# Two of four sums of weight quarters, made by adding transfers instead of by VectorE

## The reference

```python
h = rms_norm(x, norm_ffn[l])
gate, up = jnp.split(h @ w_gate_up[l], 2, axis=-1)
x = x + (jax.nn.silu(gate) * up) @ w_down[l]
```

## Time and profile before

| | us |
|---|---|
| median of three runs | 1362.07 (1361.05 to 1362.75) |
| the profiled execution, its own time | 1360.11 |
| its span in the trace | 1358.3 |
| PE busy | 1339.5 |
| DVE busy | 849.2 |
| ACT busy | 619.4 |
| POOL busy | 54.1 |

### The profile page before, as it was taken

One profiled execution on the slowest core, in us unless ns is written; L12 is line 12 of the kernel. 1 busy time (PEld: TensorE's weight loads), 2 busy tenths in 40 slices (PEclk: granted clock), 3 DMA queues, 4 the chain that ended last, 5 costly groups with the idle time before them and its releaser, 6 DMA issues. The chain is left out here.

```text
span 1358.3 us, 18018 instructions
## 1 busy us (share of the span) xinstructions
PE 1339.5 (99%) x6941; PEld 1112.0 (82%) x6941; DVE 849.2 (63%) x1313; ACT 619.4 (46%) x1145; POOL 54.1 (4%) x38
## 2 busy tenths in 40 slices
PE   9999999999999999999999999999999999999998
PEld 7888878888888888888788887888798888888886
DVE  5785654457666554344558876767565666666668
ACT  6554333457777533223426466663343332433333
POOL 0025300000000000000010000000000000000000
PEclk9999999999999999999999999999999999999999
DMA  5222213242111154322261200002325412421321
GB/s 168 86 83 81 67 59 114 88 138 80 36 59 61 63 188 151 104 91 66 87 195 61 70 17 16 32 1 78 130 88 168 142 38 87 154 94 63 113 73 62
DMA packets 33622, 120.68 MB, mean 89 GB/s; under 512 B 3716, under 2 KB 5124, under 8 KB 32258
## 3 DMA queue, kind: packets, MB, share of 16 engines
q1 hardware_dynamic: 32962, 118.48, 26.3%
q10 hardware_dynamic: 576, 1.05, 0.4%
HBM read 112.18 MB, written 4.19 MB: 86 GB/s over the span
## 5 line engine op out<-in xcount | busy, mean ns | idle before, releaser
L983 PE MATMUL bank<-a_hi,whi 128*128 128x512 f32 (+1 forms) x880 | 346.9, 394 | 0.4 <-DVE a_lo L2381 0.4
L983 PE MATMUL bank<-a_hi,wlo 128*128 128x512 f32 (+1 forms) x880 | 337.1, 383 | 0.0
L983 PE MATMUL bank<-a_lo,whi 128*128 128x512 f32 (+1 forms) x880 | 336.2, 382 | 0.0
L1431 ACT ACTIVATE whi<-wraw 128x1024 fp32r<-128x1024 f32 x170 | 176.0, 1055 | 195.6 <-PE bank L983 135.1
L1808 DVE TENSOR_TENSOR wlo<-wraw,whi 128x1024 fp32r<-128x1024 f32 x170 | 207.6, 1234 | 60.7 <-ACT whi L1431 54.7
L983 PEld LDWEIGHTS bank<-a_hi,wlo 128*128 128x128 f32 x880 | 165.5, 188 | 32.7
L983 PEld LDWEIGHTS bank<-a_hi,whi 128*128 128x128 f32 x880 | 165.9, 189 | 31.6 <-issue 2.3
L983 PEld LDWEIGHTS bank<-a_lo,whi 128*128 128x128 f32 x880 | 165.9, 189 | 31.1 <-issue 1.7
L983 PE MATMUL bank<-arena 128*128 128x128 f32 (+5 forms) x1332 | 184.9, 284 | 3.0 <-DVE arena L2032 1.5
L983 PEld LDWEIGHTS bank<-arena 128*128 128x128 f32 (+1 forms) x1332 | 163.9, 190 | 13.0 <-issue 5.3
L983 PE MATMUL bank<-whi,a_hi 128*128 128x512 f32 x288 | 115.6, 401 | 1.5 <-DVE wlo L1808 0.7
(11 more groups left out here) (272 smaller groups left out, 1866.5 us busy)
## 6 DMA issues: line engine op xcount, KB each, us to landing
wraw<-in_wblk SPq DMA_DIRECT2D x170, 512.0 KB, 3.8
arena<-in_quarters SPq DMA_DIRECT2D x8, 1024.0 KB, 7.1
arena<-in_quarters SPq DMA_DIRECT2D x4, 768.0 KB, 6.1
arena<-in_x SPq DMA_DIRECT2D x4, 512.0 KB, 6.1
arena<-in_x SPq DMA_DIRECT2D x1, 2048.0 KB, 7.7
spill<-arena SPq DMA_DIRECT2D x4, 512.0 KB, 7.8
arena<-spill SPq DMA_DIRECT2D x1, 2048.0 KB, 9.3
out<-arena SPq DMA_DIRECT2D x8, 256.0 KB, 2.0
```

The costliest lines, as they stand in the source:

```text
L983: return nc.tensor.matmul(o, lhsT, rhs, start=start, stop=stop, **kw)
L1431: A(whi[n % 2][:, cols], wraw[i][:, 0:cols.stop - cols.start], ACT.Copy).then_inc(s_hi, 1)
```

## The change

The signs of the scheme are turned so that all sums of weights become plus: t1 = b11 + b12, t3 = b12 + b22, t2 = t1 + b22, t4 = t2 + b21. SP copies b11 into the slot of t1 and b12 into the slot of t3 (COPIED); then POOL issues, for each, a transfer that adds another quarter from memory onto the slot, b12 onto t1 and b22 onto t3 (ADDED), once the copy has landed. b11, b21 and b22 are copied for themselves as well. t2 and t4 stay with DVE. The minus signs move into `hsplit` (one add and one subtraction swapped) and into `take` (which subtracts products 6 and, once, 7, and no longer product 4).  There are five copies and two adding transfers in a group instead of four copies. The copies of t1 and t3 stand together where b11's stood, b11's where b12's stood.

```diff
-QUARTERS = ("b11", "b12", "b21", "b22")
-SUMS = ("t1", "t2", "t3", "t4")
+QUARTERS = ("b11", "b21", "b22", "t1", "t3")
+COPIED = {"b11": 0, "b21": 2, "b22": 3, "t1": 0, "t3": 1}
+ADDED = {"t1": 1, "t3": 3}
+SUMS = ("t2", "t4")
...
-            sums = {6: [("tsum", group, 2)], 7: [("tsum", group, 3)]}.get(p, [])
+            sums = [("tsum", group, 1)] if p == 7 else []
...
-LAST_OF = {"b12": 7, "b22": 3, "b21": 4}
+LAST_OF = {"t1": 5, "t3": 7, "b22": 3, "b21": 4}
...
-    for c, name in zip(range(e - 4, e) if e - a == 8 else (e - 3, e - 3, e - 2, e - 1), ("b11", "b12", "b22", "b21")):
+    for c, name in zip((e - 4, e - 4, e - 3, e - 2, e - 1) if e - a == 8 else (e - 3, e - 3, e - 2, e - 2, e - 1),
+                       ("t1", "t3", "b11", "b22", "b21")):
...
-                    if name in QUARTERS:
+                    if name in ADDED:
+                        act.wait_ge(s_added[name], 16 * group + 16)
+                    elif name in QUARTERS:
                         act.wait_ge(s_raw[name], 16 * group + 16)
...
-                link(v.tensor_tensor(hsum[:, 0, :], a21, a22, ALU.add))
+                link(v.tensor_tensor(hsum[:, 0, :], a21, a22, ALU.subtract))
                 link(v.tensor_tensor(hsum[:, 1, :], hsum[:, 0, :], a11, ALU.subtract))
-                v.tensor_tensor(hsum[:, 3, :], a12, hsum[:, 1, :], ALU.subtract).then_inc(s_hsum, 1)
+                v.tensor_tensor(hsum[:, 3, :], a12, hsum[:, 1, :], ALU.add).then_inc(s_hsum, 1)
...
-                out_, left, right = (("t1", "b12", "b11"), ("t2", "b22", "t1"), ("t3", "b22", "b12"), ("t4", "t2", "b21"))[i]
+                out_, left, right = (("t2", "t1", "b22"), ("t4", "t2", "b21"))[i]
...
+            def add_quarters(n):
+
+                for group, name in QUARTERS_AT.get(n, ()):
+                    if name in ADDED:
+                        pool.wait_ge(s_raw[name], 16 * group + 16)
+                        cols = slice(0, width(PRODUCT_AT[group, 1]))
+                        pool.dma_start(raw[name][:, cols], dram["quarters"][4 * group + ADDED[name]][:, cols],
+                                       accum_op=ALU.add).then_inc(s_added[name], 16)
+
             for s in STEPS:
+                if s[0] == "gemm" and s[2] == 0:
+                    add_quarters(s[1])
```

More of the change, by code:

```diff
@@ L74 @@
 PAIR = {1: 0, 6: 0, 7: 0, 4: 0, 2: 1, 5: 1, 3: 1}
+SUBTRACTED = {(6, (0, 1)), (7, (1, 1))}
 TAKES = {1: ((0, 0),), 2: ((0, 0),), 6: ((0, 1),), 5: ((1, 1),), 7: ((1, 0), (1, 1)), 3: ((0, 1),), 4: ((1, 0),)}
-QUARTERS = ("b11", "b12", "b21", "b22")
-SUMS = ("t1", "t2", "t3", "t4")
+QUARTERS = ("b11", "b21", "b22", "t1", "t3")
+COPIED = {"b11": 0, "b21": 2, "b22": 3, "t1": 0, "t3": 1}
+ADDED = {"t1": 1, "t3": 3}
+SUMS = ("t2", "t4")
 def weave(*streams, weights=None):
@@ L293, in plan @@
             f = ff(c, a, whole)
-            sums = [("tsum", group, 0)] if c == e - 2 else []
-            steps += f[:2] + untaken + H(*unsplit) + f[2:4] + sums + f[4:]
+            steps += f[:2] + untaken + H(*unsplit) + f[2:]
             untaken, unsplit = [], [c]
-        steps[-2:-2] = [("tsum", group, 1)]
+        steps[-2:-2] = [("tsum", group, 0)]
         made = products(group, (e - a) // 2)
@@ L756, in emit @@
         hsq = mem(4, [512])
-        raw = {name: mem(kb, [BLK]) for name, kb in (("b11", 0), ("b12", 8), ("b21", 16), ("b22", 24), ("t1", 32))}
-        raw.update(t2=raw["b11"], t3=raw["b12"], t4=raw["b21"])
+        raw = {name: mem(kb, [BLK]) for name, kb in (("b11", 0), ("t3", 8), ("b21", 16), ("b22", 24), ("t1", 32))}
+        raw.update(t2=raw["b11"], t4=raw["b21"])
         half_chunk = T // 2
@@ L844, in emit @@
         s_tsum = sem("s_weights_summed")
+        s_added = {name: sem("s_quarter_added_" + name) for name in ADDED}
         s_h, s_hsum, s_hround = sem("s_hidden_made"), sem("s_hidden_summed"), sem("s_hidden_rounded")
@@ L918, in _ @@
                     cols = slice(0, width(PRODUCT_AT[group, 1]))
-                    src = dram["quarters"][len(QUARTERS) * group + QUARTERS.index(name)]
+                    src = dram["quarters"][4 * group + COPIED[name]]
                     sp.dma_start(raw[name][:, cols], src[:, cols]).then_inc(s_raw[name], 16)
@@ L1964, in tsum @@
                 r = {name: ap[:, cols] for name, ap in raw.items()}
-                out_, left, right = (("t1", "b12", "b11"), ("t2", "b22", "t1"), ("t3", "b22", "b12"), ("t4", "t2", "b21"))[i]
+                out_, left, right = (("t2", "t1", "b22"), ("t4", "t2", "b21"))[i]
                 for name in (left, right):
-                    if name in QUARTERS:
+                    if name in ADDED:
+                        dve.wait_ge(s_added[name], 16 * group + 16)
+                    elif name in QUARTERS:
                         dve.wait_ge(s_raw[name], 16 * group + 16)
@@ L1970, in tsum @@
                         dve.wait_ge(s_tsum, len(SUMS) * group + SUMS.index(name) + 1)
[L1971 to L1977, removed]
+                dve.wait_ge(s_lo, 2 * PRODUCT_AT[group, 1 if out_ == "t2" else 2] + 2)
+                v.tensor_tensor(r[out_], r[left], r[right], ALU.add).then_inc(s_tsum, 1)
             def take(n):
@@ L1987, in take @@
                         x = x2[:, 2 * rows_half + t, 512 * cols_half:512 * cols_half + 512]
-                        last = v.tensor_tensor(x, x, bank[BANK[g]][:, :], ALU.subtract if b["product"] == 4 else ALU.add)
+                        last = v.tensor_tensor(x, x, bank[BANK[g]][:, :],
+                                               ALU.subtract if (b["product"], (rows_half, cols_half)) in SUBTRACTED else ALU.add)
                     last.then_inc(s_end["V"], 1)
```

## The result

The change makes the kernel slower by a third of a percent: 1366.66 us median (1363.81 to 1367.25, ten runs) against 1360.95 (1359.7 to 1362.75, ten runs) beside it, ratio 1.0035, 95% interval 1.0025 to 1.0045. The forecast of no change was wrong; the price lies near that of the first rival. (The prediction's base of 1362.07 was a median of three runs, 1.1 us above the one of ten.)

What follows compares the result with a forecast made beforehand. PE was taken as the bound, busy 99% of the span. Terms for sums, signs, waits for adds and late weight pieces were all 0, so 1360.1 us profiled, 1362.1 for the median, forecast as 1362.0; range 1359.6 to 1366.5.

Steps and rivals of the forecast that it cites:

- the first rival: First group: adds cost three copies or more, weight pieces come late, PE waits 4.8 us, 1366.9 us; chance 0.11.
- What bounds the kernel: Feed-forward: PE, busy 99% of the span, never late until deep in the last group; only 2.0 us of waits there.
- DVE's relief is worth 0: Six removed weight sums, 12.7 us of DVE's time, lie beside PE's work: worth 0, at best 0.1 us.
- Signs 0: Additions for subtractions in `hsplit`, the sums and `take`: same instruction, same shape, 0.
- POOL's queue outside the span 0: Around the span 1.8 us lie now; nothing added, against a rival of another 1 to 3 us, chance 0.03.
- The wait for the adds is covered by 41 us: First group: t1 has at least 41 us to be made; two transfers take at most 28 us; price 0.
- An add costs two copies of engine time, 6.1 us: DMA engines: an add must read the slot besides what a copy does, so twice a copy's 3.06 us.
- The slack of the weight pieces: Block PE begins at 1050.77: second piece may be 5.1 us late, first 7.5; next block's 4.9 and 5.5.
- At 3.6 us of overhang it holds: 1030 to 1060 us: 15.3 us of added engine work exceeds 11.7 us free by 3.6, within the pieces' slack.
- 0 (weight pieces late): Term of the sum for SP's weight pieces delayed by the added bytes in all groups: 0 us.
- Two of the prediction's own signs of being wrong: PE wait for `wlo` between 1040 and 1075 us, DMA share near 1.0 there; third was DVE idle before line 1980.
- The rival "weight pieces late": First group: overhang 9.8 us less slack of about 5, PE waits 4.8 us, giving 1366.9 us; chance 0.11.

Runs made afterwards that it cites:

- e3: The change with its adding transfers left out, so both sums missing, five copies a group and two DVE sums remaining: 1360.42 us, ratio 1.0002.
- e1: The change, but the first group's two adds wait until DVE has made the rests of chunk 6's and chunk 7's weights: 1360.32 us, ratio 0.9999.
- e2: The change with both adding transfers of each group replaced by plain copies from the same queue at the same place: 1359.86 us, ratio 1.000.
- e7: The change, but in the first group the add onto t3 waits until the rests of chunk 7's weights are made: 1360.56 us, ratio 0.9996.
- e8: The change with b11's copy moved behind chunk 5's weight pieces in the first two groups: 1365.23 us, ratio 1.0029.
- e6: The kernel before, without adds; SP holds chunk 4's second weight piece until PE has ended chunk 3's block: 1367.08 us, ratio 1.0048.
- e4: The change, but the add onto t3 waits until the add onto t1 has landed: 1366.45 us, ratio 1.004.
- e5: The change with only the first group's adds; those of the second and third group left out: 1364.52 us, ratio 1.0029.

## Why the prediction was wrong

- *What bounds the kernel, and that DVE's relief is worth 0*: right (e3: 1.0002; 316.24 us without a gap before, in e1 and in e3). The six sums that went had lain beside PE's work.
- *Signs 0*: right (e1). *POOL's queue outside the span 0*: nearly. Around the span lie 1.8 to 1.9 us in e1, as before, but 2.2 in the change and 2.1 to 2.2 in e2, e7 and e8; what makes these 0.3 to 0.4 us is open.
- *The wait for the adds is covered by 41 us*: right. The adds landed after at most 15.8 us, and neither DVE's six instructions of line 1980 nor ACT ever waited for one.
- *An add costs two copies of engine time, 6.1 us*: about right, 5.1 to 6.2. The page "Collectives: The Full Stack" of the Trainium skill, section "The bandwidth ceiling: the fold count and why AG ≠ RS ≠ AR", finds about half a copy's rate for the adding step of a collective, as it reads two sources; these runs agree (1.7 to 2.1 copies).
- *The slack of the weight pieces, 5.1 us for chunk 4's second and 7.5 for its first*: right. e7 was 3.6 us late with the second and lost nothing; the change was 9.5 us late with it and PE waited 3.9 us, and 7.7 us late with the first, where PE waited 0.3.
- *"At 3.6 us of overhang it holds"*, and with it the term "0 (weight pieces late)": this step failed. It took the extra work of the engines over 30 us, took off the free share of all 30 us, and compared the rest with the slack of one piece. Of the 11.7 us free, 7.4 lay behind 1044 us, when the piece had all but landed, and only 0.9 in the 6 us in which it was on its way. What counts here is the work outstanding when the piece is issued: by the rough sum some 16 us in the change instead of 6 before (two pieces of 1.5 and a quarter of 3). Landing went from 6.1 us to 15.6, that is 9.5 later; less the slack of 5.1, 4.4, and PE waited 3.9 + 0.3. The first rival supposed in the same way that some of the lateness falls on the adds, "which nobody misses"; the small, urgent piece landed with the second add, not ahead of it. Two of the prediction's own signs of being wrong came: a PE wait for `wlo` at 1053 us, and a DMA share of 1.00. That transfers of SP and POOL share the same engines the Trainium skill says (page "DMA: Bandwidth & Descriptors", section "Issuing engines are not separate DMA queues"), and the trace agrees (with POOL's adds beside it SP's piece took 15.6 us instead of 6.1); the prediction had that rule, but not its price at one moment.
- *The rival "weight pieces late"* had mechanism, place and nearly the price: 1366.9 against 1366.66, by a sum that was right by chance. It put an add at three copies, where two do, started from a base 1.1 us too high, and had neither the clock (1.5 us in the profiled execution) nor what comes with a wait beyond its length.

Why SP's piece ends last and not by its own size is not settled. Beside plain transfers of POOL it landed late too (e2, 10.6 us), so it is nothing of the adding alone; what the adding does is to make the backlog longer. No run looks into the order within the engines.

## What to carry to other kernels

Cost an added transfer at the moment when the next urgent one is issued: sum the engine time of all that is outstanding then, and compare the end of it with the last moment at which that one may land; here that was good to some 2 us. A mean share over tens of microseconds hides a burst. A transfer that nobody waits for soon should wait for a quiet stretch by a semaphore that exists already; here two such waits removed the loss. And relief for an engine for which PE never waits was worth nothing here, so it may not cost anything either.

## What was not expected of the hardware

- An adding transfer of 1 MB took 5.1 to 6.2 us of all 16 engines and 8.7 to 15.8 us to land; a plain one from the same queue took 2.9 us of them and 5.1 to 10.5 us to land (e2).
- The full engines moved 254 GB/s with adds among them and 434 GB/s without.
- A single wait of PE costs more than its length in some executions. After the new wait of 3.9 us the granted clock was at half for about 3.3 us, after the 5.6 us of e6 for about 6.9, and after the 3.7 us of e4 it fell too; after e4's 1.6 us and e5's 1.7 us it did not. In the change and in e6 the fall cost PE 1.5 us. Of the ten executions of the change seven had a mean clock of 0.997; of the kernel before it was seven of 29 in one set and seven of 25 in the other. The old wait of 1.9 us in the last group was followed by such a fall in the profiles of the change, e1, e4 and e8 (22.3 us for 90 matmuls), and not in the others (20.8 us). That alone makes 1.5 us of scatter.
